# Attention scores: the two heads of a pair in turn, on the lower and the upper 64 rows

## The chip, the cores and the metric

One core of a Trainium2 chip runs the whole program. The metric is the time of one execution on the device, in microseconds (us), as the median of several executions. The engines of the core are named as the profile names them: PE is the matrix engine (PEld its weight loads), DVE the vector engine, ACT the scalar engine, POOL the general engine, SP the engine that starts most DMAs.

## What is computed

Two transformer blocks over 512 tokens of width 1024, in float32. The change lies in the attention of the first block, which has eight heads of 64 columns:

```python
MOBA_HEADS, MOBA_HEAD_DIM = 8, 64          # q, k, v: (B, T, H, 64), T = 512

logit = einsum('hqd,hkd->hqk', q, k) * 64 ** -0.5 - slopes[:, None, None] * dist
logit = where(dist >= 0, logit, -1e30)
p = softmax(logit, axis=-1)
out = einsum('hqk,hkd->hqd', p, v)         # times silu(z) in a later stage
```

The keys form two blocks of 256, and a query takes its own block and the earlier ones that a gate picks; with 512 tokens there is at most one earlier block and it is always picked, so each query attends to every key at or before its own place. So the kernel computes plain causal attention with a linear bias on distance.

## The kernel before

The program is a row of stages, each a block in which every engine runs its own list of instructions, and semaphores tie the lists together; between stages all engines meet at a barrier. The stage of this case is `attention` (L500). It also does a second job on PE: the last eight column chunks of the input projection (the gates z), which were left over for it by the stage before.

**Tiling.** Heads are handled in pairs: 128 rows of a tile `a_q0` or `a_k0` (pair 0) and `a_q1`, `a_k1` (pair 1) hold two heads, head b = 0 on partitions 0 to 63 and b = 1 on 64 to 127. A loop written out over two halves (`for i in range(halves)`) takes two pairs each. Within a half there are 16 steps, one for each pair p, head b and block of 128 queries qt. A query block attends to qt + 1 blocks of 128 keys, so a step is 128, 256, 384 or 512 columns wide. The list `steps` (L524) sets the order of these 16 in all engines alike.

**What one step does.** PE: `score` (L569), one matmul of 64 rows into one of three banks (0, 1, 6, by step number modulo 3), then `turn` (L576), a transpose of the probabilities for each key block, then `weigh` (L584), one matmul of 128x64 for each key block. DVE: the logits (L656, score plus slope times distance), their maximum (L660) and its negative (L661), and two steps later `normalise` (L634, L635). ACT: the exponential with its sum (L697), and `keep` (L676), the copy of the transposed probabilities out of PSUM. The matmuls are float32; each score and each `weigh` matmul shows as two records in the trace, while the projection's (L600, in float32r, three products of high and low parts) show as one.

**The projection between them.** A chunk of z takes 24 matmuls of 512 columns. `project` (L588) puts them between the attention's instructions, a chunk for four steps: none at steps n with n % 4 == 0, and eight at each of the other three, four before `turn` and four before `weigh`. After the last of them ACT copies bank 7 out (`keep_z`, L686) and splits the next chunk's weights (`high`, L682); DVE makes the low parts (`low`, L640) at n % 4 == 2.

**Order on PE around the change.** PE issues `score` two steps ahead. In iteration n it does `score(n + 2)`, half of `project(n)`, `turn(n + 1)`, the other half, `weigh(n)` (L609 to L616). `score(n)` waits until DVE is through with the logits of step n - 3 (same bank); `turn(n)` waits for the exponential of step n. On ACT, at steps with n % 4 == 0 the order is exponential n, `keep(n - 1)`, `keep_z`, and then at the next step `high`, exponential n + 1.

Of the kernel before, what the change touches and what calls it, by code (L numbers as in the profile page):

```python
# [15 lines left out]
TT = T // P  # L16
# [62 lines left out]
def after(count):  # L79

    return count + 1
# [418 lines left out]
def attention(nc, k, io, xt, proj, mixed):  # L500
# [8 lines left out]
    with ExitStack() as st:  # L509
# [11 lines left out]
        probs_t = k.sb("a_probs_t", [P, 2, T], ctx=st)  # L521
        stat = k.sb("a_stat", [P, 4, 4 * TT], ctx=st)

        steps = [(p, b, qt) for p in range(2) for b in range(2) for qt in range(TT)]  # L524
        n_steps = len(steps)
        score_bank = [k.ps[0], k.ps[1], k.ps[6]]

        def before(i, n, depth):

            return after(i * n_steps + max(n - depth + 1, 0))  # L530
# [6 lines left out]
        with nc.Block() as block:  # L537
            @block.sync
            def _(sp):
                for j, c in enumerate(z_chunks):  # L540
                    if j >= 2:
                        sp.wait_ge(w_lo[j % 2], after(j // 2))
                    sp.dma_start(raw[j % 2][:, :, :], w_dram[:, :, c * P:(c + 1) * P]).then_inc(raw_in[j % 2], 16)
# [9 lines left out]
            @block.tensor  # L553
            def _(pe):

                for t in range(TT):
                    for j in range(4):
                        mm = pe.transpose(k.ps[t][:, j * P:(j + 1) * P], proj[:, V0 + j, t * P:(t + 1) * P], k.ident[:, :])
                    mm.then_inc(v_turned, 1)
                pe.wait_ge(v_kept, after(TT))  # L560

                def score(i, n):
                    p, b, qt = steps[n]
                    pe.wait_ge(logits_made, before(i, n, 3))
                    if b == 0 and qt == 0:
                        pe.wait_ge(pair_ready, after(i * 4 + 2 * p + 2))
                    h = slice(b * A_DH, (b + 1) * A_DH)
                    w = (qt + 1) * P
                    pe.matmul(score_bank[n % 3][:, 0:w], qs[p][h, qt * P:w], ks[p][h, 0:w], start=True, stop=True).then_inc(scored, 1)  # L569

                def turn(i, n):
                    p, b, qt = steps[n]
                    pe.wait_ge(exped, after(i * n_steps + n + 1))
                    pe.wait_ge(kept_t, before(i, n, 2))
                    for kt in range(qt + 1):
                        mm = pe.transpose(k.ps[2 + n % 2][:, kt * P:(kt + 1) * P], probs[:, n % 3, kt * P:(kt + 1) * P], k.ident[:, :])  # L576
                    mm.then_inc(turned, 1)

                def weigh(i, n):
                    p, b, qt = steps[n]  # L580
                    pe.wait_ge(kept_t, after(i * n_steps + n + 1))
                    pe.wait_ge(normed, before(i, n, 2))
                    for kt in range(qt + 1):
                        mm = pe.matmul(k.ps[4 + n % 2][:, 0:A_DH], probs_t[:, n % 2, kt * P:(kt + 1) * P],  # L584
                                       vtok[:, kt, bass.ds(i * (2 * P) + p * P + b * A_DH, A_DH)], start=(kt == 0), stop=(kt == qt))
                    mm.then_inc(weighted, 1)

                def project(i, n, part):  # L588

                    q, r = n // quarters, n % quarters  # L590
                    if r == 0:
                        return
                    j, b = z_of(i, q), z_of(i, q) % 2
                    if r == 1 and part == 0:
                        pe.wait_ge(w_lo[b], after(j // 2 + 1))
                        pe.wait_ge(z_kept, after(j))
                    at = (r - 1) * 8 + part * 4
                    for m in range(at, at + 4):
                        c, (w, x) = m // 3, ((whi, hi), (whi, lo), (wlo, hi))[m % 3]
                        mm = pe.matmul(k.ps[7][:, :], w[b][:, c, :], x[:, c, :], start=(m == 0), stop=(m == 3 * DC - 1))  # L600
                    if r == quarters - 1 and part == 1:
                        mm.then_inc(z_product, 1)

                for i in range(halves):

                    score(i, 0)
                    score(i, 1)
                    turn(i, 0)
                    for n in range(n_steps):  # L609
                        if n + 2 < n_steps:  # L610
                            score(i, n + 2)
                        project(i, n, 0)
                        if n + 1 < n_steps:
                            turn(i, n + 1)
                        project(i, n, 1)
                        weigh(i, n)  # L616
# [1546 lines left out]
def build(nc, io, out):  # L2163
    with ExitStack() as ctx:
# [7 lines left out]
        with ExitStack() as st:  # L2172
# [10 lines left out]
            with ExitStack() as st2:  # L2183
                xt = (k.sb("xt_hi", [P, DC, T], F32R, ctx=st2), k.sb("xt_lo", [P, DC, T], F32R, ctx=st2))
                project_first(nc, k, io, xt, w8, proj, gates)
                k.end_stage()
                attention(nc, k, io, xt, proj, mixed)
                k.end_stage()
# [69 lines left out]
```

## Time and profile before

| | us |
|---|---|
| median of 3 runs | 2431.01 |
| lowest and highest of them | 2428.66 and 2432.61 |
| the profiled execution | 2433.4 |
| its span in the trace | 2431.6 |

Times inside the program are counted from the start of the span. The attention stage's own work, from its barrier to the next stage's first instruction, lies between about 203 and 333 us; it is some 5% of the span. The rows of the trace name an instruction by its line, its engine, the tile that it writes and those that it reads. "64\*128" on a PE row is the part of the array that the weights take (64 rows, 128 columns), and "x2" the number of records merged into a row.

### The profile page before, as it was taken

To read this page: it belongs to the slowest core of one execution; us is meant where nothing else is said; L and a number is where in the kernel's file an instruction comes from. 1 tells how busy PE (TensorE), PEld (TensorE's weight loads), DVE (VectorE), ACT (ScalarE), POOL (GpSimd) and SP (SyncE) were. 2 spreads that over 40 slices of the span, in tenths; PEclk is the share of its full clock that TensorE was granted. 3 is DMA by queue.
4 is the path that set the end of the run, shared out by engine and by line. 5 is a ranking of instruction groups with operands and counts; after the bars stand their busy time and mean duration, and the time that the engine had idled before them with its cause. 6 is when DMAs were issued, how large, how long until landed. Compare 5 with 4: busy or idle time off the path is not lost. (4 is left out here: it accounts for less than half of the span.)

```text
span 2431.6 us, 36275 instructions
## 1 busy us (share of the span) xinstructions
PE 2165.9 (89%) x11207; PEld 1893.3 (78%) x11207; DVE 1692.8 (70%) x3352; ACT 818.5 (34%) x1408; POOL 774.4 (32%) x677
## 2 busy tenths in 40 slices
PE   3996988764999998797869999999998999999997
PEld 2874678653777776686869999999997888888885
DVE  2475545536686764489568888888875888888887
ACT  3443332203223221422424444444432333333333
POOL 2000034000000000046547878878753222222220
PEclk8997889886999999898989999999999999999999
DMA  4422100022332422511336878878688999999995
GB/s 106 85 53 43 28 1 1 0 78 72 87 100 74 114 54 70 166 51 45 119 135 227 273 251 290 284 254 279 225 283 302 335 337 337 336 339 338 337 338 208
DMA packets 229901, 428.88 MB, mean 176 GB/s; under 512 B 18468, under 2 KB 155844, under 8 KB 229572
## 3 DMA queue, kind: packets, MB, share of 16 engines
q1 hardware_dynamic: 172228, 254.97, 33.9%
q0 software_dynamic: 41472, 151.01, 18.0%
q10 hardware_dynamic: 16128, 22.03, 2.5%
q8 instruction: 34, 0.56, 0.1%
q14 instruction: 39, 0.32, 0.0%
HBM read 381.80 MB, written 46.14 MB: 176 GB/s over the span
## 5 line engine op out<-in xcount | busy, mean ns | idle before, releaser
L2132 PE MATMUL bank<-xt_hi 128*128 128x512 f32 x768 | 302.2, 393 | 10.0 <-DVE xt_lo L2061 10.0
L1852 PE MATMUL bank<-xt_hi,u_hi 128*128 128x384 f32 x896 | 309.3, 345 | 0.0
L1852 PE MATMUL bank<-xt_hi,u_lo 128*128 128x384 f32 x896 | 300.6, 336 | 0.0
L1852 PE MATMUL bank<-xt_lo,u_hi 128*128 128x384 f32 x896 | 300.2, 335 | 0.0
L2132 PE MATMUL bank<-xt_hi,xt_lo 128*128 128x512 f32 x768 | 299.8, 390 | 0.0
L2132 PE MATMUL bank<-xt_lo,xt_hi 128*128 128x512 f32 x768 | 299.8, 390 | 0.0
L1714 POOL DMA_INDIRECT row_slot<-in_peer_v_dram,row_index x128 | 140.6, 1099 | 390.7 <-DVE row_x L2065 372.7
L2108 ACT ACTIVATE xt_hi<-xh 128x1024 fp32r<-128x1024 f32 x128 | 135.8, 1061 | 339.1 <-PE bank L2132 332.8
L1383 POOL TENSOR_TENSOR k_wlo<-k_raw,k_whi 128x2048 fp32r<-128x2048 f32 x4 | 18.4, 4600 | 619.2 <-ACT k_whi L1503 619.2
L2058 DVE TENSOR_TENSOR xt_lo<-xh,xt_hi 128x1024 fp32r<-128x1024 f32 x128 | 156.9, 1226 | 84.0 <-ACT xt_hi L2108 82.6
L1793 POOL TENSOR_TENSOR u_two<-u_match,u_weight_hi 128x512 fp32r<-128x512 f32 x96 | 180.2, 1877 | 97.4 <-DVE u_match L1879 96.8
L1263 PE MATMUL bank<-xt_hi,x_whi 128*128 128x512 f32 x448 | 180.2, 402 | 21.7 <-DVE x_h L1248 10.9
L2132 PEld LDWEIGHTS bank<-xt_hi 128*128 128x128 f32 x768 | 144.8, 189 | 42.3 <-DVE xt_lo L2061 7.8
L1263 PE MATMUL bank<-xt_lo,x_whi 128*128 128x512 f32 x448 | 176.1, 393 | 0.0
L1263 PE MATMUL bank<-xt_hi,x_wlo 128*128 128x512 f32 x448 | 176.1, 393 | 0.0
L1943 ACT ACTIVATE xh<-bank 128x384 f32<-128x384 f32 x112 | 55.0, 491 | 341.7 <-PE bank L1852 338.9
L1852 PEld LDWEIGHTS bank<-xt_lo,u_hi 128*128 128x128 f32 x896 | 169.1, 189 | 0.0
L2132 PEld LDWEIGHTS bank<-xt_lo,xt_hi 128*128 128x128 f32 x768 | 144.8, 189 | 31.0 <-issue 1.2
L1852 PEld LDWEIGHTS bank<-xt_hi,u_hi 128*128 128x128 f32 x896 | 168.9, 188 | 0.0
L1852 PEld LDWEIGHTS bank<-xt_hi,u_lo 128*128 128x128 f32 x896 | 168.5, 188 | 0.0
L2132 PEld LDWEIGHTS bank<-xt_hi,xt_lo 128*128 128x128 f32 x768 | 144.7, 188 | 30.3
L1871 DVE TENSOR_TENSOR u_lo<-bank,u_hi 128x512 fp32r<-128x512 f32 x226 | 145.7, 686 | 32.4 <-ACT u_hi L1928 31.2
(430 smaller groups left out, 4924.2 us busy)
## 6 DMA issues: line engine op xcount, KB each, us to landing
xh<-in_peer_v_dram SPq DMA_DIRECT2D x128, 512.0 KB, 5.5
xh<-in_peer_u_dram SPq DMA_DIRECT2D x113, 512.0 KB
x_raw<-in_w_in_dram SPq DMA_DIRECT2D x56, 512.0 KB, 5.5
v_ga<-acts SPq DMA_DIRECT2D x128, 192.0 KB
acts<-xh ACTq DMA_DIRECT2D x112, 192.0 KB
weights<-u_spread POOLq DMA_DIRECT2D x32, 512.0 KB
v_gg<-weights SPq DMA_DIRECT2D x128, 128.0 KB
p_raw<-in_w_in_dram SPq DMA_DIRECT2D x12, 1024.0 KB
```

What stands on the lines that cost most here:

```text
L1263: mm = pe.matmul(k.ps[n][:, :], w[n][:, c, :], x[:, c, :], start=(c == 0 and w is whi and x is hi), stop=(c == DC - 1 and w is wlo))
L1383: eng.tensor_tensor(wlo[b][:, :, :], raw[sec % 2][:, :, :], whi[b][:, :, :].bitcast(F32), ALU.subtract).then_inc(w_lo[b], 1)
L1714: pool.indirect_dma_start(rows["slots"][n % SLOTS][:, :], None, io_rows, bass.IndirectOffsetOnAxis(ap=rows["index"][:, n:n + 1], axis=0)). ...
L1793: pool.tensor_tensor(two[b][:, :, h, :], match[:, :, :], part.unsqueeze(2).to_broadcast([P, TOK_TILE, P]), ALU.mult).then_inc(two_done, 1)
L1852: mm = pe.matmul(k.ps[4 + b][:, 0:DENSE], w[b][:, c, :], x[:, c, 0:DENSE], start=(c == 0 and w is uhi and x is hi), stop=(c == DC - 1 and ...
L1871: dve.tensor_tensor(ulo[b][:, 4 * f:4 * f + 4, :], k.ps[2 * b + f][:, :].rearrange("p (c n) -> p c n", c=4), uhi[b][:, 4 * f:4 * f + 4, :] ...
L1943: act.activation(ga[b], k.ps[4 + b][:, 0:DENSE], ACT.Gelu_apprx_tanh).then_inc(s["ga_done"][b], 1)
L2058: dve.tensor_tensor(vlo[b], raw[u], vhi[b].bitcast(F32), ALU.subtract).then_inc(slot_v[u], 1)
L2108: act.activation(vhi[b], raw[u], ACT.Copy).then_inc(s["vhi_done"][b], 1)
L2132: mm = pe.matmul(k.ps[q][:, :], h[b][:, t * P:(t + 1) * P], v[b][:, f], start=False, stop=False, skip_group_check=True)
```

## The change

The list of steps runs over query blocks outside and heads inside, so that steps n (even) and n + 1 are the two heads of a pair at the same query block and the same width. The scores of such two steps are issued one behind the other, at even n, so `score(n + 3)` is issued an iteration earlier than it was. Since `h` picks the partitions, the first of the two reads partitions 0 to 63 and the second 64 to 127. Nothing else is edited: the projection, the banks, the depth of the buffers and the waits are as they were, and the number of instructions of each kind and width is the same. But each engine's list follows `steps`, so the widths come in another order everywhere: 128, 128, 256, 256, 384, 384, 512, 512 instead of 128, 256, 384, 512 twice.

```diff
-        steps = [(p, b, qt) for p in range(2) for b in range(2) for qt in range(TT)]
+        steps = [(p, b, qt) for p in range(2) for qt in range(TT) for b in range(2)]
...
                     for n in range(n_steps):
-                        if n + 2 < n_steps:
+                        if n % 2 == 0 and n + 2 < n_steps:
                             score(i, n + 2)
+                            score(i, n + 3)
                         project(i, n, 0)
                         if n + 1 < n_steps:
                             turn(i, n + 1)
```

PE at the start of a half, before the change: iteration 0 and the start of iteration 1. `a_k0,a_q0` marks a score, `ident,a_probs` a transpose, `a_vtok,a_probs_t` a weighing, `xt_hi,a_whi0` the projection.

```order
L569 MATMUL bank0<-a_k0,a_q0 128x128
L569 MATMUL bank1<-a_k0,a_q0 128x256
L576 MATMUL bank2<-ident,a_probs 128x128
L569 MATMUL bank6<-a_k0,a_q0 128x384
L576 MATMUL bank3<-ident,a_probs 128x128 x2
L584 MATMUL bank4<-a_vtok,a_probs_t 128x64
L569 MATMUL bank0<-a_k0,a_q0 128x512
L600 MATMUL bank7<-xt_hi,a_whi0 128x512
```

The same place after the change:

```order
L569 MATMUL bank0<-a_k0,a_q0 128x128
L569 MATMUL bank1<-a_k0,a_q0 128x128
L576 MATMUL bank2<-ident,a_probs 128x128
L569 MATMUL bank6<-a_k0,a_q0 128x256
L569 MATMUL bank0<-a_k0,a_q0 128x256
L576 MATMUL bank3<-ident,a_probs 128x128
L584 MATMUL bank4<-a_vtok,a_probs_t 128x64
L600 MATMUL bank7<-xt_hi,a_whi0 128x512
```

The projection now starts right behind the first weighing, and the four scores ahead of it have 768 columns in place of 1280.

PE around step 4, the first step without projection in the steady part, before the change (weigh 3, score 6, turn 5, weigh 4, score 7, then the projection's next chunk):

```order
L584 MATMUL bank5<-a_vtok,a_probs_t 128x64 x4
L569 MATMUL bank0<-a_k0,a_q0 128x384
L576 MATMUL bank3<-ident,a_probs 128x128 x2
L584 MATMUL bank4<-a_vtok,a_probs_t 128x64
L569 MATMUL bank1<-a_k0,a_q0 128x512
L600 MATMUL bank7<-xt_hi,a_whi1 128x512
```

The same place after the change (weigh 3, scores 6 and 7, turn 5, weigh 4, the projection):

```order
L584 MATMUL bank5<-a_vtok,a_probs_t 128x64 x2
L569 MATMUL bank0<-a_k0,a_q0 128x512
L569 MATMUL bank1<-a_k0,a_q0 128x512
L576 MATMUL bank3<-ident,a_probs 128x128 x3
L584 MATMUL bank4<-a_vtok,a_probs_t 128x64 x3
L600 MATMUL bank7<-xt_hi,a_whi1 128x512
```

The weighing ahead is half as long, a pair of 512 columns each stands ahead of the turn, and no score behind it.

ACT at the same steps, before the change (exponential 4, `keep` 3, `keep_z`, `high`, exponential 5, `keep` 4):

```order
L697 ACTIVATE a_probs,a_stat<-a_logits,a_stat 128x128
L676 ACTIVATE a_probs_t<-bank3 128x512
L686 ACTIVATE proj<-bank7 128x512
L682 ACTIVATE a_whi0<-a_raw0 128x1024
L697 ACTIVATE a_probs,a_stat<-a_logits,a_stat 128x256
L676 ACTIVATE a_probs_t<-bank2 128x128
```

and after it:

```order
L698 ACTIVATE a_probs,a_stat<-a_logits,a_stat 128x384
L677 ACTIVATE a_probs_t<-bank3 128x256
L687 ACTIVATE proj<-bank7 128x512
L683 ACTIVATE a_whi0<-a_raw0 128x1024
L698 ACTIVATE a_probs,a_stat<-a_logits,a_stat 128x384
L677 ACTIVATE a_probs_t<-bank2 128x384
```

The copy and the split between the two exponentials stay where they were; the exponential behind them is 384 wide instead of 256.

## Rows read from the trace of the kernel before

**Rows 1.** The page: the span, and PE's granted clock in 40 slices, in tenths.

```profile
span 2431.6 us, 36275 instructions
...
PEclk8997889886999999898989999999999999999999
```

**Rows 2.** Stretches: length, then busy time (instructions) of each engine, clock, DMA.

```profile
207.00:332.00 125.00, 110.09 (x497) 79.35 (x496) 63.18 (x178) 45.14 (x113) 0.00 (x0) 0.87 0.18 33
...
239.60:252.50 12.90, 12.46 (x64) 9.13 (x62) 7.42 (x21) 5.47 (x15) 0.00 (x0) 1.00 0.26 43
...
225.00:227.00 2.00, 2.00 (x10) 1.64 (x8) 0.04 (x1) 0.18 (x1) 0.00 (x0) 0.64 0.65 147
...
280.00:284.00 4.00, 4.00 (x14) 3.19 (x12) 1.13 (x3) 1.30 (x3) 0.00 (x0) 0.50 0.60 104
...
294.00:296.00 2.00, 2.00 (x5) 1.12 (x4) 1.96 (x5) 0.97 (x3) 0.00 (x0) 0.68 0.00 0
296.00:298.00 2.00, 2.00 (x8) 1.56 (x7) 1.07 (x3) 0.83 (x3) 0.00 (x0) 0.50 0.00 0
```

**Rows 3.** Waits from 207 to 332 us: who for whom, total, times, longest.

```profile
DVE a_stat L634 <- PE bank L584: 46.5, 24, 3.5
...
PE bank L576 <- ACT a_probs L697: 3.9, 7, 1.0
```

**Rows 4.** Timeline around step 4: start, length, engine, line, operands [idle before].

```profile
232.99 1.00 PE L584 MATMUL bank<-a_vtok,a_probs_t 128*128 128x64 f32 x8
233.19 0.60 ACT L686 ACTIVATE proj<-bank 128x512 f32<-128x512 f32 x1 [3.73 <-PE bank L600]
233.68 1.05 ACT L682 ACTIVATE a_whi<-a_raw 128x1024 fp32r<-128x1024 f32 x1
...
233.92 0.91 PE L569 MATMUL bank<-a_k,a_q 64*128 64x384 f32 x2
...
234.62 0.50 ACT L697 ACTIVATE a_probs<-a_logits,a_stat 128x256 f32<-128x256 f32 x1
...
235.27 0.44 PE L576 MATMUL bank<-ident,a_probs 128*128 128x128 f32 x2 [0.44 <-ACT a_probs L697]
```

**Rows 5.** Timeline of PE, a weighing with a score behind it, and one without.

```profile
242.47 0.78 PE L584 MATMUL bank<-a_vtok,a_probs_t 128*128 128x64 f32 x6
243.17 0.70 PE L569 MATMUL bank<-a_k,a_q 64*128 64x256 f32 x2
243.80 0.50 PE L600 MATMUL bank<-xt_lo,a_whi 128*128 128x512 f32 x1
244.13 0.39 PE L600 MATMUL bank<-xt_hi,a_wlo 128*128 128x512 f32 x1
...
311.87 0.48 PE L569 MATMUL bank<-a_k,a_q 64*128 64x128 f32 x2
...
326.49 0.78 PE L584 MATMUL bank<-a_vtok,a_probs_t 128*128 128x64 f32 x6
327.08 0.48 PE L600 MATMUL bank<-xt_lo,a_whi 128*128 128x512 f32 x1
327.40 0.40 PE L600 MATMUL bank<-xt_hi,a_wlo 128*128 128x512 f32 x1
```

**Rows 6.** Timeline of PE, the second half's first two scores (128 and 256 columns).

```profile
272.58 0.89 PE L569 MATMUL bank<-a_k,a_q 64*128 64x128 f32 x4 [1.40 <-DVE a_k L651]
```

**Rows 7.** Groups by form, 207 to 332 us: operands, count, busy us, mean ns.

```profile
L569 PE MATMUL bank<-a_k,a_q 64*128 64x512 f32 x16 | 10.9, 765 | 0.0
...
L697 ACT ACTIVATE a_probs<-a_logits,a_stat 128x384 f32<-128x384 f32 x8 | 4.9, 615 | 9.9 <-DVE a_stat L661 9.9
...
L697 ACT ACTIVATE a_probs<-a_logits,a_stat 128x256 f32<-128x256 f32 x8 | 4.0, 496 | 0.0
...
L697 ACT ACTIVATE a_probs<-a_logits,a_stat 128x128 f32<-128x128 f32 x8 | 3.2, 402 | 18.9 <-DVE a_stat L661 18.9
```

**Rows 8.** Timeline of PE, the first projection matmul of the stage.

```profile
221.94 0.79 PE L600 MATMUL bank<-xt_hi,a_whi 128*128 128x512 f32 x1
```

## The prediction

> **What bounds the kernel now.** I read the page first, for size: the span is 2431.6 us [rows 1], and the stage that the change touches takes about 125 of it [rows 2]. Everything outside lies behind barriers and keeps its instructions, so only those 125 us can change, by the time from the stage's first score to its last normalising. To be told from no change, the result has to move by more than 0.2%, that is 4.9 us.
>
> Next the stretches [rows 2]: over the stage PE is busy 110 of 125 us, DVE 63, ACT 45. In one block of four steps (239.6 to 252.5) PE is busy 12.46 of 12.9 us at the full clock. The waits [rows 3] name DVE behind PE for 46.5 us, which is idle time of an engine with time to spare, and PE behind ACT for only 3.9 us in 7 places. So PE's own list of instructions sets the pace, except at one place in four steps. That place is in [rows 4]: at the steps without projection, PE has a weighing and a score and then sits idle 0.44 us until the exponential comes. ACT has there, one after the other, the copy of bank 7 (from 233.19), the split (1.05 us) and the exponential. From the weighing's start (232.99) to the turn (235.27) it is 2.28 us. I call this stretch the opening; a half has three (steps 4, 8 and 12). In it ACT is the bound, elsewhere PE.
>
> **What a score costs PE.** Compare a weighing of six records with a score behind it and one without [rows 5], from the weighing's start to the second projection matmul: 244.13 - 242.47 = 1.66 us against 327.40 - 326.49 = 0.91 us. A lone score of 256 columns costs 0.75 us. How much of that is streaming? A lone 128 lasts 0.48 and a lone 256 0.70 us [rows 5], so 0.21 to 0.22 us go to each 128 columns; I take 0.21, and 0.42 for 256. The remaining 0.33 us is what it costs to go from the 128-row matmuls to a 64-row one and back. It does not recur between two scores of the same rows: the first two of a half, 128 and 256 columns, take 0.89 us together [rows 6], only 0.41 more than the lone 128. So lone scores cost 0.54, 0.75, 0.97 and 1.18 us for 128 to 512 columns, and a score right behind another costs its streaming alone, 0.21, 0.42, 0.64 or 0.85.
>
> **The unknown: the second score's other rows.** No row of the trace has two neighbouring matmuls on different halves of the rows. Let x be the part of the second one's streaming that stays on PE. The upper bound from a row is x = 1, no overlap, as on the same rows [rows 6]; the lower is x = 0, fully beside the first. I take x = 0.5: a score is two records (16 for 8 scores of 512 columns [rows 7]), which share their rows and run in order, A1 A2 B1 B2. Only B1 has a neighbour on the other rows, A2, so at best half of the second score goes under the first.
>
> The Trainium skill ("TensorEngine Tiling (Array Packing)", Tiling Modes) says that different tiles run in parallel and that only a change of the tiling mode, not of the tile, drains the engine. By its plain reading the second score would cost nothing, and the sum would be the one for x = 0 below; the 0.33 us of a lone score agrees with its word on the drain, while no run so far shows two tiles side by side.
>
> **The change part by part, for one half, at the full clock.** PE's time outside the openings:
> - Scores before: 4 x (0.54 + 0.75 + 0.97 + 1.18) = 13.76; less three of 384 columns inside the openings (2.91) and the 0.33 that the first pair already saves: 10.52 us.
> - Scores after: outside the openings stand the first ones of five pairs (128 twice, 256, 384 twice), 0.54 x 2 + 0.75 + 0.97 x 2 = 3.77, and their seconds, x times (0.42 + 0.42 + 1.28 = 2.12). With x = 0.5: 4.83 us.
> - Weighing: 40 key blocks in either order, at 0.93 / 4 = 0.23 us each [rows 4]. Ahead of the openings' turns stood 4 + 4 + 4, now 2 + 4 + 2. Four more are outside: +0.92.
>
> The openings: before 3 x 2.28 = 6.84. ACT's chain keeps its copy and split; only the exponential changes from 256 columns (0.50 us) to 384 (0.615) at steps 4 and 12 and to 128 (0.40) at step 8 [rows 7]: 2.40, 2.40 and 2.19 us, together 6.99. Does PE now need longer? At steps 4 and 12 it has a weighing of two blocks, 0.46, a first score of 512 columns, about 1.12 to its end, and 0.85x: 2.0 us for x = 0.5, 2.43 for x = 1. At step 8: 0.93 + 0.70 + 0.42x, at most 2.05. So for x = 0.5 ACT stays the bound, and what the pairing saves in there turns into idle time. The openings cost +0.15.
>
> New small waits, my estimate from the durations above: behind each opening's turn the weighing waits for a wider `keep`, some 0.1 us three times; at the end of a half, turn 15 now waits for a chain on DVE (normalise, `low`, then logits 15 at 512 columns, which stood at the other end of the block before), some 0.4. Together +0.7. The wait of score n + 3 for the logits of step n costs nothing: exponential n is done already, since turn n came before. Issued early, it queues ahead of turn n + 1, which is counted above. DVE and ACT have as much work as before and PE has less of it to hide them under, but with 63 and 45 of 125 us [rows 2] they bind only in the openings.
>
> Sum for a half: 4.83 + 0.92 + 0.15 + 0.7 - 10.52 = -3.9 us; two halves **-7.8 us**.
>
> **The clock.** Each half begins at half clock (0.50 at 280 to 284, and 0.64 at 225 to 227, where it rises) [rows 2]. In this trace the rise at about 226.5 comes 4.6 us after the first projection matmul at 221.94 [rows 8]. In the new order the projection starts about 2 us sooner. The rise could come earlier by up to one such interval or not at all; one interval of 3.3 us at half clock is what the fall at 294.6 to 298 took ((1 - 0.68) x 2 x 2 + 2 [rows 2]), and costs 1.65 us. Falls such as that one can also come or go. I take none of it, and keep 1.65 us for each half in the range.
>
> **Against the runs.** The profiled execution took 2433.4 us, 2.4 above the median. It becomes 2433.4 - 7.8 = 2425.6, and the median 2431.0 - 7.8 = **2423.2 us**.
>
> **The rivals.**
> - *No overlap (x = 1).* The switch is saved, the streaming is not. Scores outside 5.89, openings 2 x 2.43 + 2.19 = 7.05, +0.21: 5.89 + 0.92 + 0.21 + 0.7 - 10.52 = -2.8 for a half, **-5.6**, so 2425.4. For it: [rows 6] is all that the trace shows of neighbours. Against: the two use other rows and other banks.
> - *Full overlap (x = 0).* 3.77 + 0.92 + 0.15 + 0.7 - 10.52 = -5.0, **-10.0**, so 2421.0. For it: nothing in the trace; against: a score's two records share their rows [rows 7].
> - *The change does not do what it says:* going from the lower to the upper rows costs the 0.33 us of a change of shape again. To x = 1 come 5 x 0.33 = 1.65 outside and, in the openings, 2 x 0.33 at steps 4 and 12 and 2.38 - 2.19 = 0.19 at step 8, together 2.5. A half gains 0.3, the whole **-0.6**, so 2430.4.
> - *Slower.* The change of rows empties the array and stops the loads of weights, so that each of 16 pairs pays more than a lone score does. It decides from (0.6 + 4.9) / 16 = 0.34 us on top of 0.33; at 0.7 us in all it gives about +5, 2436. Against: the dearest change between unlike neighbours in the rows is 0.33 us [rows 5].
>
> **How the numbers follow.** Half overlap 0.40, no overlap 0.25, full overlap 0.12, change of rows as dear as a change of shape 0.15, dearer 0.08. The range: full overlap with a rise of the clock gained in each half, 2421.0 - 3.3 = 2417.7, to the case of -0.6 with one fall more, 2432. Faster by over 0.2% means below 2426.1: most of half overlap (0.34), half of no overlap (0.13), full overlap (0.11), a little of the fourth: 0.60. Slower 0.08, the rest 0.32.
>
> **What would show it.** In the trace after: a pair of 512 columns lasts about 1.55 us in its four records if x is 0.5, 1.95 if 1, 1.15 if 0; B1 starts before A2 ends by the length of its streaming. The opening from weighing to turn is still 2.2 to 2.4 us, with PE idle some 0.4 in it. The stage takes about 117 us in place of 125. The projection starts at about 219.8. I am wrong if PE idles elsewhere (a chain on DVE), if the opening grows, or if the stage shortens and the time does not.

## The result: 15 us faster, 0.64%, twice what was forecast

| | us |
|---|---|
| kernel before, median of 4 runs | 2429.84 (2427.35 to 2432.61) |
| changed kernel, median of 4 runs | 2414.76 (2410.91 to 2416.82) |
| ratio | 0.9936, 95% interval 0.9919 to 0.9953 |
| forecast | 2423.2, range 2417.7 to 2432.0 |
| profiled execution of the change | 2416.8, span 2415.1 |

The direction was right, the size was not: the time lies below the range. The page after, against [rows 1]: the span and PE's granted clock in 40 slices.

```profile
span 2415.1 us, 36275 instructions
...
PEclk8997999887999998898989999999998999999998
```

The stage itself, from its first score to the end of its last normalising, in three profiles of each kernel (the second and third of each are the runs e9, e10, e0 and e11 below). Columns as in [rows 2]: stretch, length, busy time of PE, PEld, DVE, ACT, POOL, mean clock, DMA. First the kernel before, three executions:

```profile
214.78:330.61 115.83, 109.97 (x496) 79.31 (x496) 60.31 (x173) 42.80 (x111) 0.00 (x0) 0.89 0.16 28
```

```profile
214.60:329.23 114.63, 108.01 (x496) 78.19 (x496) 60.37 (x173) 42.80 (x111) 0.00 (x0) 0.91 0.16 28
```

```profile
215.01:330.93 115.92, 110.05 (x496) 79.38 (x496) 60.30 (x173) 42.84 (x111) 0.00 (x0) 0.89 0.16 28
```

then the changed one:

```profile
218.74:320.68 101.94, 92.72 (x496) 71.48 (x496) 59.95 (x173) 41.91 (x111) 0.00 (x0) 0.92 0.18 32
```

```profile
215.62:317.19 101.57, 92.36 (x496) 71.19 (x496) 59.95 (x173) 41.89 (x111) 0.00 (x0) 0.92 0.19 32
```

```profile
217.71:318.19 100.48, 91.30 (x496) 70.37 (x496) 59.94 (x173) 41.92 (x111) 0.00 (x0) 0.93 0.19 32
```

The length falls from 115.5 to 101.3 us on average, by 14.1. PE's busy time falls by 17 us (from 109.3 to 92.1), DVE's and ACT's by less than 1 us, and PE's busy share from 95 to 91%. The waits in the stage after the change (203 to 322 us) say the same: against [rows 3] PE waits longer for ACT, and DVE less for PE.

```profile
DVE a_stat L635 <- PE bank L584: 32.4, 22, 3.0
...
PE bank L576 <- ACT a_probs L698: 7.2, 10, 1.4
```

So nearly the whole gain is in the stage. Over the whole program the medians differ by 15.1; the rest of the program, outside the stage, took 2305.7 to 2315.8 us in the profiles without following the kernel, so the last microsecond can't be placed. Among this rest is the landing of the stage's first weights: the first score comes at 214.6 to 215.0 us before, at 215.6 to 218.7 after, and at 214.0 to 215.3 in e1 to e3. Two of these, e1 and e3, issue the same instructions as the changed kernel up to there. So it varies by some microseconds with the execution; three profiles of each kernel are too few to tell whether the change has a part in it.

**The two things that made it.** First, the pair of scores. Around step 4, where [rows 4] stood before, the changed kernel shows:

```profile
233.25 0.55 PE L584 MATMUL bank<-a_vtok,a_probs_t 128*128 128x64 f32 x4
233.45 0.60 ACT L687 ACTIVATE proj<-bank 128x512 f32<-128x512 f32 x1 [2.50 <-PE bank L600]
233.73 0.30 PEld L569 LDWEIGHTS bank<-a_k,a_q 64*128 64x128 f32 x4
233.73 1.13 PE L569 MATMUL bank<-a_k,a_q 64*128 64x512 f32 x4
...
233.94 1.05 ACT L683 ACTIVATE a_whi<-a_raw 128x1024 fp32r<-128x1024 f32 x1
...
234.89 0.60 ACT L698 ACTIVATE a_probs<-a_logits,a_stat 128x384 f32<-128x384 f32 x1
...
235.64 0.55 PE L576 MATMUL bank<-ident,a_probs 128*128 128x128 f32 x3 [0.78 <-ACT a_probs L698]
```

Two scores of 512 columns, four records (x4), last 1.13 us. That is what the prediction took for one lone score (1.12). Narrower looks at the same place, from 233.74 to 233.80 and from 234.5 to 234.6 us, show how:

```profile
233.73 0.70 PE L569 MATMUL bank<-a_k,a_q 64*128 64x512 f32 x2
```

```profile
234.27 0.59 PE L569 MATMUL bank<-a_k,a_q 64*128 64x512 f32 x2
```

The four records run two and two: a pair starts at 233.73, the next pair at 234.27. Since records on the same rows follow one another (e3 below), each pair has one record of either score: both first records, then both second ones. In the prediction's terms x is 0, not 0.5. The opening, from weighing (233.25) to turn (235.64), is 2.39 us; forecast was 2.40. PE sits idle in it for 0.78 us, where x = 0 gives 2.40 - 1.58 = 0.82.

Second, the clock. From the trace's record of the granted clock I add up the time at the lower level (1.2 GHz) within the stage, and take half of it off the length. This is an estimate of the stage at the full clock (2.4 GHz): in the trace before, the projection's matmuls follow each other in 0.43 us at the lower level (222.53, 222.96, 223.38) and in 0.23 at the full one (227.53, 227.76, 227.99). It takes PE for the bound throughout, and e4, e7 and e8 test it below. "First rise" is counted from the first score, "second" is the stretch at the start of the second half, "in between" one in the middle of a half.

| profile | length | at the lower level | first rise after | second | in between | length less half |
|---|---|---|---|---|---|---|
| before | 115.8 | 25.3 | 11.7 | 10.2 | 3.4 | 103.2 |
| before, e9 | 114.6 | 21.4 | 11.1 | 6.8 | 3.4 | 104.0 |
| before, e10 | 115.9 | 25.4 | 11.8 | 10.2 | 3.4 | 103.2 |
| change | 101.9 | 15.8 | 9.0 | 6.8 | 0 | 94.1 |
| change, e0 | 101.6 | 15.3 | 8.4 | 6.8 | 0 | 94.0 |
| change, e11 | 100.5 | 13.6 | 6.8 | 6.8 | 0 | 93.7 |

At the full clock the change is worth 103.4 - 93.9 = 9.5 us, and the time at the lower level goes from 24.0 to 14.9 us, worth 4.6. Together 14.1. Every execution has a mean granted clock on record, over the whole program, and it points the same way: 0.9500 on average in 8 of the changed kernel, 0.9476 in 34 of the kernel before on the three chips used below, which would be some 11 us less at the lower level. Outside the stage this time varies by itself (224 to 248 us in the six profiles), so this alone would prove nothing.

### The profile page after: what moved, and what is told of

The parts are those of the page before. It is cut to its first block and busy times, and to the rows that moved or that the text cites. A ratio compares the mean times of both kernels' runs of the same rounds, so it can differ in the third digit from the quotient of the medians.

```text
span 2415.1 us, 36275 instructions
## 1 busy us (share of the span) xinstructions
PE 2143.7 (89%) x11207; PEld 1880.5 (78%) x11207; DVE 1690.7 (70%) x3352; ACT 817.7 (34%) x1408; POOL 770.8 (32%) x677
```

## The experiments

Theory T: the gain is made of saved switches between 128-row and 64-row matmuls, of the second score running wholly beside the first, and of less time at the lower clock. Rivals: the order of widths brings it; the neighbourhood alone brings it; overlap is worth nothing, because ACT's chain in the openings swallows it; the clock's part is chance. Medians of runs below are against the kernel before on the same chip; e0 to e3 shared a chip (before 2428.7), e4 to e7 another (before 2429.1), e8 to e11 a third (before 2426.8).

### e0: the changed kernel again

> The changed kernel again, beside the three others on the same chip. Expected 2412 to 2417 us, 14 to 16 us below before; its profile also tells whether the first weights of the stage land as late as in the first profile (first score at 218.7 us against 214.8 before). Theory: that landing varies from run to run, and has nothing to do with the change; then it differs here from 218.7 by a microsecond or more.

Measured: 2413.53 us (2412.43 to 2415.95), ratio 0.9931 (0.9914 to 0.9948). The first score came at 215.62, three microseconds earlier than in the first profile of the same kernel, and the stage's length is the same within 0.4 us. The result stands. That the landing varies is seen; that the change has no part in it is not shown by this.

### e1: the order alone

```diff
-                        if n % 2 == 0 and n + 2 < n_steps:
+                        if n + 2 < n_steps:
                             score(i, n + 2)
-                            score(i, n + 3)
```

> The changed order of steps (heads inside, query blocks outside) with the scores issued singly, one in each iteration, as before. Theory: the gain of 15 us comes from the two scores of a pair running at the same time on the two halves of the rows, which needs them to be neighbours. Then this one shows 32 lone scores again, stays within 3 us of the kernel before (2427 to 2433 us), and a 512-column score still takes about 1.1 us on its own. Rival: the order of widths, by which the projection starts sooner and the clock rises sooner, brings the gain. Then it shows half of it or more, 2422 us or less.

Measured: 2434.88 us (2433.0 to 2438.6, 10 runs), ratio 1.0023 (1.0014 to 1.0033): slower than before, by 6 us, and 21 us slower than the change. The order of widths brings nothing by itself; that rival is out. But my expectation of 2427 to 2433 was missed too, and the profile says why. The stage:

```profile
214.01:336.46 122.45, 113.78 (x496) 82.14 (x496) 60.97 (x173) 42.53 (x111) 0.00 (x0) 0.86 0.15 26
```

PE around step 4:

```profile
231.44 1.12 PE L569 MATMUL bank<-a_k,a_q 64*128 64x512 f32 x2
233.35 0.55 PE L576 MATMUL bank<-ident,a_probs 128*128 128x128 f32 x3 [0.78 <-ACT a_probs L697]
233.73 0.88 PE L584 MATMUL bank<-a_vtok,a_probs_t 128*128 128x64 f32 x6
234.54 1.80 PE L569 MATMUL bank<-a_k,a_q 64*128 64x512 f32 x2
236.27 0.79 PE L600 MATMUL bank<-xt_hi,a_whi 128*128 128x512 f32 x1
```

and the stretches at its end and behind it:

```profile
232.00:235.00 3.00, 2.22 (x12) 1.35 (x11) 1.94 (x6) 2.38 (x6) 0.00 (x0) 0.97 0.00 0
235.00:242.00 7.00, 7.00 (x21) 4.79 (x20) 2.92 (x5) 1.90 (x6) 0.00 (x0) 0.52 0.39 66
```

Both 512-column scores stand in the same step without projection. From 231.44 to 236.27 us PE has no 512-column matmul on all rows, and the clock falls at 234.9 for 6.8 us. The stage has 34.5 us at the lower level, 10 more than before (some 5 us of time), and is 105.2 us long less half of it, 1.8 more than before. So in this order the pairing does not only save time, it also repairs the opening.

### e2: neighbours in the old order

```diff
-                        if n + 2 < n_steps:
+                        if n % 2 == 0 and n + 2 < n_steps:
                             score(i, n + 2)
+                            score(i, n + 3)
```

> The old order of steps with the new issue: two scores next to each other, but of one head, so both on the same 64 rows, and of widths 128 with 256 and 384 with 512. It saves the 0.33 us of going to a 64-row matmul and back, and overlaps nothing. Theory (overlap is most of the gain): 3 to 7 us faster than before, 2423 to 2427 us, and a pair of 384 and 512 columns takes about 1.8 us in its four records. Rival (the neighbourhood alone is what matters): 2415 to 2418 us.

Measured: 2420.62 us (2418.74 to 2422.19), ratio 0.9964 (0.9949 to 0.9978): 8.1 us faster than before, more than I expected of it and 7 us short of the change. The stage and two pairs, of 384 with 512 columns and of 128 with 256:

```profile
214.78:322.75 107.97, 103.79 (x496) 77.13 (x496) 59.80 (x173) 42.76 (x111) 0.00 (x0) 0.90 0.17 30
```

```profile
233.37 1.77 PE L569 MATMUL bank<-a_k,a_q 64*128 64x384 f32 x4
...
238.30 0.92 PE L569 MATMUL bank<-a_k,a_q 64*128 64x128 f32 x4
```

On the same rows the two run one behind the other (1.77 against the 0.91 of a lone 384 [rows 4]; 0.92 against the 0.89 of [rows 6]). The pairing also fills the opening: PE no longer idles before the turn at 235.07. Length less half the time at the lower level is 97.0, 6.5 less than before: two thirds of the 9.5 us can be had without the second set of rows, in the old order.

### e3: the same kernel, both scores on the same rows

```diff
-                    h = slice(b * A_DH, (b + 1) * A_DH)
+                    h = slice(0, A_DH)
```

> The changed kernel with one thing undone: the second score of each pair reads the lower 64 rows too, so it computes the first head's scores again and the second head's are left out. Order, widths, banks, waits and the number of instructions are those of the changed kernel. Theory (overlap): the two run one after the other, a pair of 512 columns takes 1.95 us instead of 1.13, and the whole is 3 to 8 us slower than the changed kernel, 2418 to 2423 us. By the recorded prediction's case without overlap it should be 5.6 us faster than before, some 2424. Rival (overlap is worth nothing, since the openings absorb it): the same as the changed kernel, 2413 to 2416 us.

Measured: 2419.68 us (2418.45 to 2421.00), ratio 0.9956 (0.9940 to 0.9973). All four runs lie above all four of e0 on that chip; the difference of the medians is 6.2 us.

```profile
215.26:321.10 105.84, 101.07 (x496) 77.03 (x496) 60.11 (x173) 41.92 (x111) 0.00 (x0) 0.93 0.18 31
```

```profile
231.15 1.98 PE L569 MATMUL bank<-a_k,a_q 64*128 64x512 f32 x4
233.06 0.55 PE L576 MATMUL bank<-ident,a_probs 128*128 128x128 f32 x3
```

A pair of 512 columns takes 1.98 us in place of 1.13, and the time at the lower clock is the same (15.3 us here and in e0). So the second set of rows is worth 105.8 - 101.6 = 4.3 us in the stage. The prediction's sums for x = 1 and x = 0 differ by 10.0 - 5.6 = 4.4. With the stages less half their time at the lower level, the change can be added up in three steps: the order alone costs 1.8 us (e1), the neighbourhood takes off 7.0 (105.2 to 98.2, e3), the other rows 4.3 more. The rival that the openings swallow the overlap is out: they do swallow their share (0.78 us of idling instead of none), which the sum had counted.

### e6: how PE orders the records

Ahead of the first half's scores, five groups of unused score matmuls, each followed by four full ones:

```diff
+                def probe(bank, half, w):
+                    h = slice(half * A_DH, (half + 1) * A_DH)
+                    pe.matmul(k.ps[bank][:, 0:w], qs[0][h, 0:P], ks[0][h, 0:w], start=True, stop=True)
...
+                for group in (((6, 1, T),), ((0, 0, T), (1, 0, T), (6, 1, T)), ((0, 0, T), (6, 1, T), (1, 0, T), (5, 1, T)),
+                              ((0, 0, T), (6, 1, P)), ((0, 0, P), (6, 1, T))):
```

> The changed kernel with a probe ahead of the first half's scores, its results unused: five groups of score matmuls, each between full matmuls: one alone on the upper rows; lower, lower, upper; lower, upper, lower, upper; lower 512 columns with upper 128; lower 128 with upper 512. It asks how PE orders the two records of a float32 matmul. Theory A (each half of the rows has its own order, so all records of a half follow each other and the halves run side by side): lower, lower, upper takes two scores' time (about 1.95 us at full clock), with the upper one's first record starting beside a record of the first or the second lower one; four alternating take 1.95 as well. Theory B (the two records of a score are interleaved with the neighbour's only where the two scores are of the same width): 512 with 128 takes 1.3 us or more rather than 1.15. For the whole: 10 to 14 us slower than the changed kernel.

The five groups (L610) and what follows them (L606), all at the full clock:

```profile
227.27 1.12 PE L610 MATMUL bank<-a_k,a_q 64*128 64x512 f32 x2
228.32 1.20 PE L606 MATMUL bank<-xt_hi 128*128 128x512 f32 x4
229.45 1.98 PE L610 MATMUL bank<-a_k,a_q 64*128 64x512 f32 x6
231.36 1.19 PE L606 MATMUL bank<-xt_hi 128*128 128x512 f32 x4
232.48 1.99 PE L610 MATMUL bank<-a_k,a_q 64*128 64x512 f32 x8
234.40 1.19 PE L606 MATMUL bank<-xt_hi 128*128 128x512 f32 x4
235.52 1.12 PE L610 MATMUL bank<-a_k,a_q 64*128 64x512 f32 x4
236.57 1.19 PE L606 MATMUL bank<-xt_hi 128*128 128x512 f32 x4
237.69 1.13 PE L610 MATMUL bank<-a_k,a_q 64*128 64x128 f32 x4
```

Narrower looks at the second group (lower, lower, upper), from 229.5 to 229.9, from 230.1 to 230.35 and from 231.0 to 231.2 us:

```profile
229.45 0.71 PE L610 MATMUL bank<-a_k,a_q 64*128 64x512 f32 x2
```

```profile
229.45 1.14 PE L610 MATMUL bank<-a_k,a_q 64*128 64x512 f32 x4
```

```profile
230.84 0.59 PE L610 MATMUL bank<-a_k,a_q 64*128 64x512 f32 x1
```

The slot to the next full matmul is 1.05 us for one score, 1.91 for lower, lower, upper, 1.92 for four scores in turn, 1.05 and 1.06 for 512 columns with 128, in either order. In the second group two records run from 229.45 on, four have started by 230.35, and the last two start alone, at 230.41 and 230.84. If the three scores ran in the order written and only neighbours overlapped, the upper one could not start before the second lower one, at 230.41; but from there on one record starts at a time, the second lower score's. The trace does not name a record's rows; but two scores on the same rows never run side by side (e3), so the upper score, third in the list, started together with the first. In this probe each half of the rows takes its own matmuls in its own order and does not wait for the other half. Theory A holds, B (only equal widths interleave) is out. The single execution took 2440.6 us, some 26 more than the changed kernel and not the 10 to 14 expected: the stage's own first score came at 240.2 us, 22 to 25 later than in the profiles of the change.

### e4 and e7: PE kept at work, after and before

```diff
+                def keep_warm(count):
+                    for _ in range(count):
+                        pe.matmul(k.ps[4][:, :], hi[:, 0, 0:P], hi[:, 0, :], start=True, stop=True)
...
                 for i in range(halves):
-
+                    if i:
+                        pe.wait_ge(normed, after(i * n_steps - 1))
+                    keep_warm(5 if i else 18)
                     score(i, 0)
                     score(i, 1)
+                    keep_warm(3)
                     turn(i, 0)
```

> The changed kernel with PE kept at work where it waits: 18 projection-like matmuls of 128 rows and 512 columns, results unused, ahead of the first score, 5 ahead of the second half's first score, 3 behind the first two scores of each half. Theory (the 4.8 us that the x = 0 sum leaves over are the granted clock): of the 15 to 16 us at half clock that the changed kernel has between its first score and its last normalising, 8 or more go, and each is worth half of itself: the stage's length falls from 101.6 to some 96 to 98 us, the whole to 2407 to 2411 us. Rival (the clock's share is chance, the half-clock stretches come back elsewhere): 2412 to 2416 us with 13 us or more at half clock.

> The kernel before with the same unused matmuls in the same places. Theory: with the clock taken out of both, the change is worth what it takes off PE's list at full clock, 9 to 10 us in the stage: this one lies at 2417 to 2422 us, 9 to 10 us above the changed kernel kept warm, not 15. Rival (the 15 us are all overlap and saved switches, the clock has no part in the difference): 14 to 16 us above it.

Measured: e4 2413.57 us (2409.26 to 2417.47), e7 2425.92 (2421.36 to 2431.46, 10 runs; ratio 0.9984, 0.9973 to 0.9994). The stage of e4, then of e7:

```profile
216.62:314.52 97.90, 91.29 (x507) 69.83 (x507) 59.77 (x173) 41.91 (x111) 0.00 (x0) 0.98 0.19 33
```

```profile
215.89:327.70 111.81, 107.92 (x507) 77.99 (x507) 60.20 (x173) 42.69 (x111) 0.00 (x0) 0.94 0.16 29
```

In e4 3.4 us at the lower level are left and the stage is down to 97.9 us, as expected; but the whole is no faster than the change (2413.5), which I had expected at 2407 to 2411. Its runs scatter over 8 us, and its first score came a microsecond later than e0's. From the end of the stage to the end of the program its profile has 2097.6 us, where the three of the change have 2094.0 to 2097.1 and the three of the kernel before 2091.1 to 2101.0. A rest that varies by so much can hide 3.7 us; whether it does stays open. In e7 the same matmuls left 13.7 us at the lower level. Both fall at 217.1, but e4 rises again after 3.4 us and e7 after 10.2, and e7 falls once more, at 278.6, at the start of the second half. So neither expectation for the difference was met: it is 12.4 us, 13.9 in the stage. Less half of the lower clock it is 104.98 - 96.19 = 8.8, near the 9.5 above (both with the added matmuls in it). Given the same help, the changed list has 10 us less at the lower level than the old one, in one profile of each.

These runs also test the halving. Eleven of the added matmuls stand inside the stage, some 2.6 us at 0.235 each. Put on the change's 93.9 and the old kernel's 103.4 at the full clock they give 96.5 and 106.0; e4 and e7 have 96.2 and 105.0. So a difference between two kernels that is worked out in this way is good to about a microsecond.

### e5 and e8: an earlier start

In e5 the first half's scores no longer wait for the projection's first weights; e8 adds the unused matmuls of e4, 2 in place of 18.

```diff
-                low(0)
...
+                        if i == 0 and n == 1:
+                            low(0)
                         if n >= 2:
                             normalise(i, n - 2)
...
-                high(0)
...
-                        if n % quarters == 1 and j + 1 < len(z_chunks):
+                        if j == 0:
+                            if n >= 2:
+                                high(n - 2)
+                        elif n % quarters == 1 and j + 1 < len(z_chunks):
                             high(j + 1)
```

> The changed kernel with one thing moved: the first half's scores no longer wait for the first projection weights. DVE makes q and k before its low part of chunk 0 (which goes behind step 1's maximum), and ACT does the split of chunks 0 and 1 ahead of exponentials 2 and 3. The first score then comes at 208 to 209 us instead of 214 to 218; the projection still waits for the landing (211.6 to 215.6) and two splits. Expected 3 to 5 us faster than the changed kernel: 2409 to 2412 us. Rival (the projection's weights set the end in any case, the early scores only wait in PSUM): 0 to 1 us.

> The early start of the first half (e5) together with unused matmuls that keep PE at work: 2 ahead of the first score, 5 ahead of the second half's first score, 3 behind the first two scores of each half. Theory: the fall of the clock at the start of the second half (some 7 us at half clock in every run of the changed order so far) goes, worth some 3.4 us less 1 to 2 us for the added matmuls that do not fit into waits: 1 to 3 us faster than e5, 2409 to 2411 us, stage 101 to 103 us from a first score at 209. Rival: as e5, 2412 us.

Measured: e5 2412.08 us (2409.66 to 2412.40), ratio 0.9936 (0.9920 to 0.9953); e8 2410.08 (2408.84 to 2411.46), ratio 0.9937 (0.9921 to 0.9954). The stages:

```profile
209.11:313.22 104.11, 93.44 (x496) 71.58 (x496) 61.06 (x174) 43.10 (x112) 0.00 (x0) 0.92 0.20 37
```

```profile
209.06:310.96 101.90, 92.46 (x507) 70.90 (x507) 60.98 (x174) 43.07 (x112) 0.00 (x0) 0.97 0.20 38
```

The scores start at 209.1, and the stage ends at 313.2 and 311.0 us, where the change ended at 317.2 to 320.7. In e5 the projection's first matmul comes 5.6 us behind the first score:

```profile
214.75 0.79 PE L600 MATMUL bank<-xt_hi,a_whi 128*128 128x512 f32 x1 [1.35 <-DVE a_wlo L641]
```

That is 5.2 us sooner than in e0 (219.97), and the stage ends 4.0 us sooner. But e5's median is only 1.4 us below e0's (on another chip), less than the 3 to 5 expected; the rest of the program varies by more than this, and the runs do not tell. In e8 the lower level at the start of the second half is gone, as expected, and the stage is 2.2 us shorter than e5's in spite of the added matmuls (less half of the lower level 98.5 against 95.6, for 2.6 us of added matmuls); its lower median is from another chip, where the kernel before is lower too. Both ratios are the change's ratio within the intervals: that either beats the changed kernel is not shown.

### e9, e10 and e11: more profiles of both kernels

> The kernel before, for a second profile. Theory: its 25 us at half clock between first score and last normalising are typical (20 to 29), because each half starts cold and its projection starts late; its stage length less half of that stays at 103.2 us within 0.5. Rival: the 25 us were chance, and another execution has 16 or less.

> The kernel before, for a third profile, with the same expectation: 20 to 29 us at half clock in the stage, and 103.2 us within 0.5 once half of these are taken off.

> The changed kernel, for a third profile: 12 to 19 us at half clock in the stage (15.9 and 15.3 so far), and a stage length of 94.0 us within 0.5 once half of these are taken off.

Measured: the rows and the table in the section on the result. The time at the lower level was 21.4 and 25.4 us (before) and 13.6 (change), inside what was expected; the lengths less half were 104.0, 103.2 and 93.7, of which 104.0 misses the 103.2 within 0.5.

## Why the prediction was wrong, point by point

**What bounds the stage: right.** PE's list, except in the openings. An opening was forecast at 2.40 us for steps 4 and 12 and measured at 2.39 at step 4, at 2.19 for step 8 and measured at 2.17; the new small wait at turn 15 was put at 0.4 and was 0.24 and 0.51 in the two halves:

```profile
263.99 0.66 PE L576 MATMUL bank<-ident,a_probs 128*128 128x128 f32 x4 [0.24 <-ACT a_probs L698]
```

```profile
311.95 0.66 PE L576 MATMUL bank<-ident,a_probs 128*128 128x128 f32 x4 [0.51 <-ACT a_probs L698]
```

**What a score costs: right.** The sum for x = 1 was 5.6 us; with both scores on the same rows (e3) the stage at the full clock is 103.4 - 98.2 = 5.2 us shorter than before. The rivals in which a change of rows is as dear as a change of shape, or dearer, are out: it costs nothing that the trace shows.

**The overlap: wrong, and the first step that failed.** The prediction set x = 0.5 from "a score is two records, which share their rows and run in order, A1 A2 B1 B2. Only B1 has a neighbour on the other rows". PE's list has the scores in that order, but PE does not keep it across the two halves of the rows: the records run as A1 with B1, A2 with B2 (e6, and the narrow rows above). So x = 0. This was a rival with a chance of 0.12 and the sum of 10.0 us; measured at the full clock are 9.5. It was the plain reading of the Trainium skill's sentence ("TensorEngine Tiling (Array Packing)", Tiling Modes), that different tiles run in parallel, and the trace agrees with it. I had set an argument of my own, on the order of records, above it, and no row spoke for that order: [rows 7] shows that there are two records, not how two scores' records mix. Of the missing 7.3 us this step accounts for 9.5 - 7.8 = 1.7.

**The clock: wrong, and the larger error.** "I take none of it" was the term; by the halving above it measured 4.6 us. The prediction had seen that the projection starts sooner. It does: 4.35 us behind the first score (223.09) in place of 7.16 [rows 8].

```profile
223.09 0.77 PE L600 MATMUL bank<-xt_hi,a_whi 128*128 128x512 f32 x1
```

The rise comes 6.8 to 9.0 us after the first score instead of 11.1 to 11.8, and it follows the projection's start by about as much as before (2.5 to 4.6 us, before 4.0 to 4.6). The prediction named two more places, the start of the second half and falls that can come or go, and put both at nothing. The second half's start gains 0 to 3.4 us. And the fall in the middle of a half, at 294.7 us in the first profile, is not confined to one execution: each of the three profiles of the old kernel has one such fall (in e9 at 249.6), none of the three of the new one has. On average over the three profiles of each, the first rise gives 3.5 us less at the lower level, the second half's start 2.3, the falls 3.4, and half of that is time. In front of its fall the old kernel has 3.9 us without a projection matmul, from the weighing's start to the projection's, with two lone scores and 0.44 us of idling in them; the change has 3.5 us at steps 4 and 12 (233.25 to 236.71) and less at step 8. e1, with 4.8 us from its score's start to the projection at step 4, has falls at three of its openings, at 234.9, 251.9 and 265.6 us. That shorter openings are the cause of the missing falls would fit most of this, but no run changed an opening's length alone, and two things speak against length as the whole cause: the fall at 251.9 in e1 comes behind an opening with only 3.2 us between two projection matmuls (the change has 3.3 at step 4, the old kernel 3.7), and e7, whose openings are as long as the old kernel's, has no fall in the middle of a half. The cause stays open. e3 and e2 show that it is not the overlap: e3 has no such fall either, and e2, with its full pairs on the same rows, has none.

**The range.** It reached 2417.7 by x = 0 and one sooner rise in each half, 3.3 us in all. The median went to 2414.8, beyond that, by the falls in the middle of a half (1.7 us), by a microsecond outside the stage, and because the kernel before, measured with it, has its median at 2429.8 where the range was counted from 2431.0. Of the 7.3 us by which the forecast gain (7.8) falls short of the measured one (15.1), 1.7 are the overlap, 4.6 the clock and 1.0 is not placed.

## What to carry to other kernels

Two float32 matmuls of 64 rows (here of 128 to 512 columns), on different halves of the rows and next to each other in PE's list, cost one: price the second at zero, add what is saved by going to the small shape once and not twice (0.33 us here), and then look what else was waiting for PE, since part of it turns into idling. Where a stage starts at the lower clock, as this one, an edit that brings the full matmuls forward and the small ones together can be worth time at the clock too, here by estimate half as much as the direct saving; count the time at the lower clock in several profiles of the old kernel before setting that term to zero. An unfavourable order and a favourable pairing can be two halves of one edit: the order alone cost 6 us, and with the pairing the same order is part of a gain of 15.

## What the runs showed of the hardware that I had not expected

- The two halves of PE's rows each take their matmuls in order, but not in order with each other: a score third in the list started with the first (229.45 us in e6), and lower, lower, upper took 1.91 us, as long as two scores.
- A score of 128 columns beside one of 512 costs nothing, whichever comes first (1.05 and 1.06 us to the next full matmul, as for one alone).
- The four weight loads of a pair are done within 0.30 us of its start (the PEld row of the opening), and the pair lasts 1.13 us where a lone score lasts 1.12.
- The clock fell in e1 at 234.9 us, after 3.0 us (232 to 235) in which PE was busy for 2.22, with transposes, 64-column matmuls and lone scores.
